# The first expert team's upward products, expert by expert, with the ring slots given back one at a time

## The chip, the cores and the metric

The kernel runs on one core of one Trainium2 chip. The metric is the time of one execution on the device in microseconds (us); lower is better.

## What is computed

One layer on 256 tokens of width 2048, all in float32: an attention and retention mixer, which the change does not touch, and then a mixture of experts. Each token chooses one of 4 groups and in it the best 2 of 8 experts, so there are 32 experts with three matrices each (`w1`, `w3`: 2048 x 512, `w2`: 512 x 2048), 12.6 MB an expert and about 403 MB in all. The part that matters, cut from the reference:

```
h = rms_norm(x, norm2_g)
a = jnp.einsum('nd,edf->nef', hf, w1)
b = jnp.einsum('nd,edf->nef', hf, w3)
y = jnp.einsum('nef,efd->nd', jax.nn.silu(a) * b * comb[..., None], w2)
```

`comb` is zero but for a token's two experts. The kernel computes each expert only for the tokens that chose it, in 32 slots.

## The kernel before

**Teams.** The experts are computed in 8 teams of 4 (`TEAM`), each expert with 32 token slots (`SLOTS`), so that a team fills 128 slots. The weights of a team come in 24 transfers of 2 MB (128 partitions x 4096 float32), numbered k = 0 to 23. Transfers 0 to 3 are the first half (q = 0) of `w1` of the four experts, 4 to 7 the first half of `w3`, 8 to 11 and 12 to 15 the second halves (q = 1) of `w1` and `w3`, and 16 to 23 are `w2` (two groups of four). They go into a ring of 8 slots; for the first team three further buffers (`extra`) hold transfers 8 to 10.

**The queue.** All of them are issued in this order by SyncE (L352, in `load`). Before each it waits for the semaphore `ring_used`, which counts transfers that TensorE has done with. In the first team transfer 11 waits for `ring_used` >= 1, transfer 12 for 2, ..., 18 for 8, and transfers 19 to 23 wait for 12 to 16; transfer k of a later team `it` waits for `it * 24 + k - 7`, so that of the second team, which is number 24 in the count of the whole stream, waits for 17.

**A team on TensorE.** `gather` picks the rows of the normalised input that belong to the slots by products with a 0/1 matrix `pick_p` (L1448, four parts j of four 128-column chunks; ScalarE copies each part to `h_e`, L703). `up` multiplies `h_e` by `w1` into bank 0 and by `w3` into bank 1: the stationary operand is 128 x 32 (the 32 slots of one expert), the moving one 128 x 512 (all inner columns of that expert). The four experts of the team write to four groups of 32 output partitions, so that four products with different weights are in the array side by side. Each product of float32 operands appears as two weight loads and two matmuls in the trace. The loop takes all four experts of a chunk before the next chunk, and gives back four transfers together:

```
last.then_inc(ring_used, TEAM)
```

ScalarE then makes the silu (L728, scaled by the slot's reciprocal root mean square, which TensorE gathers at L1442), VectorE the product `hm` (L1153), TensorE turns `hm` (L1499) and runs `down` (L1517) with `w2`, again four experts side by side. In the order of TensorE's program the gathering for the next team lies between a team's `up` and its `down` (`between`). The order for the first team, in `first_team`, is: `gather` 0 and 1, `up` q = 0, `gather` 2 and 3, `up` q = 1, `between`.

**The columns.** Row p*4+j of `w2` lies on partition p, so the inner columns of `hm` are read in four classes j, every fourth column, before they are turned:

```
hm.rearrange("p (j q) -> p j q", j=J), ps[:, 1, :].rearrange("p (q j) -> p j q", j=J)
```

**VectorE before the first gathering.** `pick_tokens(0)` makes `pick_p` (L1106), which is what `gather` waits for, after the ranks (L1093). The reciprocal of the root (L1110) comes after it.

Of the kernel before, what the change touches and what calls it, by code (L numbers as in the profile page):

```python
# [32 lines left out]
ALU = mybir.AluOpType  # L33
# [3 lines left out]
P = 128  # L37
SEQ, D = 256, 2048
TH = SEQ // P
C = D // P  # L40
# [6 lines left out]
J = FF // P  # L47
# [4 lines left out]
NB = 512  # L52
# [3 lines left out]
SLOTS = 32  # L56
TEAM = P // SLOTS
# [29 lines left out]
SSQ, RSTD, QKS, QKR, MU, VAR, M8, NEG, SUM, RCP, RETS, RETR, EPS_AT, SSQ2, RSTD2, SLOT_RSTD = (  # L87
    0, 2, 4, 24, 44, 48, 52, 68, 84, 100, 116, 132, 148, 150, 158, 160)
# [13 lines left out]
def build(nc, x, norm1_g, w_in, q_norm_g, k_norm_g, idx_k_ln_w, idx_k_ln_b, ret_norm_g, w_out,  # L102
          norm2_g, w_group, w_router, w1, w3, w2, consts, out):
    ctx = ExitStack()
    with ctx:
# [22 lines left out]
        side_buf = sb("side_buf", [P, 8192])  # L128
# [12 lines left out]
        st = sb("st", [P, 162])  # L141
# [69 lines left out]
        gate_T = side_buf[:, 4608:4864]  # L211
        e_sb = side_buf[:, 4864:5376]
        hm = side_buf[:, 5376:5888]
        hm_T = side_buf[:, 5888:6400].rearrange("p (j s) -> p j s", j=J)


# [15 lines left out]
        ring_used = sem("ring_used")  # L232
# [253 lines left out]
        def _(act):  # L486
# [231 lines left out]
            def slot_rstd(it):  # L718
                act.wait_ge(gather_done, it * 4 + 4)
                nc.scalar.copy(st[:, SLOT_RSTD:SLOT_RSTD + 1], ps[:, 7, 0:1]).then_inc(slot_rstd_ready, 1)  # L720

            slot_rstd(0)

            def activate(it):

                act.wait_ge(slot_rstd_ready, it + 1)
# [39 lines left out]
        def _(v):  # L766
# [322 lines left out]
                                    idxf[:, :, 1, 0:2].unsqueeze(3).broadcast_to([P, TH, 2, EXPERTS]), ALU.is_equal))  # L1089
            V.tensor_tensor(sel, oh[:, :, 0, :], oh[:, :, 1, :], ALU.add).then_inc(sel_ready, 1)  # L1090
            v.wait_ge(sel_ready, 1)
            v.wait_ge(ranks_done, 1)
            ordered(V.scalar_tensor_tensor(posm, ps[:, 1, 0:2 * EXPERTS].rearrange("p (t e) -> p t e", t=TH), 1.0, sel,  # L1093
                                           ALU.add, ALU.mult))
# [8 lines left out]
            def pick_tokens(g):  # L1103

                it, col = slots(posm, g)
                V.tensor_tensor(pick_p, col, it, ALU.is_equal).then_inc(pick_ready, 1)  # L1106

            pick_tokens(0)
            v.wait_ge(root_done, 2)
            V.reciprocal(st[:, RSTD2:RSTD2 + TH], st[:, RSTD2:RSTD2 + TH]).then_inc(rstd_ready, 1)  # L1110
            v.wait_ge(rstd_ready, 3)
            for th in range(TH):
                V.tensor_scalar(g_in[:, th, :], ps[:, 4 + th, EXPERTS:GATES], r2[th], None, ALU.mult)
                V.tensor_scalar(small[:, th, 0:1], top8[:, th, 0, 0:1], -1.0, r2[th], ALU.mult, ALU.mult)
# [21 lines left out]
            v.sem_inc(gate_turned, 1)  # L1136
            v.sem_inc(gate_T_ready, 1)

            def team(it, more=True, scattering=True):

                v.wait_ge(gate_turned, it + 1)
                i, col = slots(posm, it)
                V.tensor_tensor(gate_p, col, i, ALU.is_equal).then_inc(pick_step, 1)  # L1143
                v.wait_ge(pick_step, it + 1)
                V.tensor_tensor(gate_p, gate_p, slots(comb, it)[1], ALU.mult).then_inc(gate_ready, 1)
                v.wait_ge(gather_done, it * 4 + 4)
                if more:
                    pick_tokens(it + 1)
                if scattering:
                    add_scattered(it)  # L1150

                v.wait_ge(silu_done, it + 1)
                V.scalar_tensor_tensor(hm.rearrange("p (j q) -> p j q", j=J), ps[:, 1, :].rearrange("p (q j) -> p j q", j=J),  # L1153
                                       st[:, SLOT_RSTD:SLOT_RSTD + 1], e_sb.rearrange("p (q j) -> p j q", j=J),
                                       ALU.mult, ALU.mult).then_inc(hm_ready, 1)
# [14 lines left out]
                    xo = acc[:, th, n * NB:(n + 1) * NB]  # L1170
                    V.tensor_tensor(xo, xo, ps[:, 3 - s % 2, :], ALU.add).then_inc(added, 1)

            team(0, scattering=False)
            v.wait_ge(acc_ready, TH)
            with v.Fori(1, TEAMS - 1) as it:
                team(it)
# [11 lines left out]
        def _(pe):  # L1188
# [245 lines left out]
            mm(ps[:, 6, 0:EXPERTS], ones, sel[:, 0, :], start=True, stop=False)  # L1434
            mm(ps[:, 6, 0:EXPERTS], ones, sel[:, 1, :], start=False, stop=True).then_inc(totals_done, 1)

            def gather(g, j):

                if j == 3:
                    pe.wait_ge(rstd_ready, 3)  # L1440
                    for th in range(TH):
                        mm(ps[:, 7, 0:1], pick_p[:, th].rearrange("p e s -> p (e s)"), st[:, RSTD2 + th:RSTD2 + th + 1],  # L1442
                           start=(th == 0), stop=(th == TH - 1))
                for c in range(4 * j, 4 * j + 4):
                    cols = slice(c // 8 * 1024, (c // 8 + 1) * 1024)
                    for th in range(TH):
                        rows = xs[:, th, cols].rearrange("p (q c) -> p c q", c=8)[:, c % 8, :]
                        last = mm(ps[:, 2 + j % 2, (c % 4) * P:(c % 4 + 1) * P], rows,  # L1448
                                  pick_p[:, th].rearrange("p e s -> p (e s)"), start=(th == 0), stop=(th == TH - 1))
                last.then_inc(gather_done, 1)  # L1450
# [22 lines left out]
            def landed_now(it, k):  # L1473
                pe.wait_ge(landed[chunk_slot(k)], it * (16 * TEAM_CHUNKS // RING) + chunk_landed(k))
                return ring[:, chunk_slot(k), :]

            def up(it, q, here=None):

                pe.wait_ge(h_e_ready, it * 4 + (2 * q + 2))
                for up in range(2):  # L1480
                    ks = [(2 * q + up) * TEAM + m for m in range(TEAM)]
                    w = [here(k) if here else landed_now(it, k) for k in ks]
                    for cc in range(8):
                        c = 8 * q + cc
                        for m in range(TEAM):
                            part = slice(SLOTS * m, SLOTS * (m + 1))
                            last = mm(ps[part, up, :], h_e[:, c, part], w[m][:, cc * NB:(cc + 1) * NB],  # L1487
                                      start=(c == 0), stop=(c == C - 1))
                    last.then_inc(ring_used, TEAM)

            def ups(it):
                up(it, 0)
# [16 lines left out]
            def down(it, halves, here=None):  # L1509
                for half in halves:  # L1510
                    ks = [UP_CHUNKS + TEAM * half + m for m in range(TEAM)]
                    w = [here(k) if here else landed_now(it, k) for k in ks]
                    for j in (2 * half, 2 * half + 1):
                        for n in range(4):
                            for m in range(TEAM):
                                part = slice(SLOTS * m, SLOTS * (m + 1))
                                last = mm(ps[part, 4 + n, :], hm_T[:, j, part],  # L1517
                                          w[m][:, j % 2 * D + n * NB:j % 2 * D + (n + 1) * NB],
                                          start=(j == 0), stop=(j == J - 1))
                    last.then_inc(ring_used, TEAM)  # L1520

            def first_team():

                pe.wait_ge(pick_ready, 1)
                for j in range(2):
                    gather(0, j)
                up(0, 0, landed_first)
                for j in (2, 3):
                    pe.wait_ge(h_e_ready, j - 1)
                    gather(0, j)  # L1530
                up(0, 1, landed_first)
                between(0, landed_first)

            def team(it):
                ups(it)
                pe.wait_ge(added, it * 8 + 16)
                between(it)
# [91 lines left out]
```

## Time and profile before

| what | value |
|---|---|
| median of 3 runs | 1373.95 us (1373.59 to 1374.65) |
| the profiled execution, its own time | 1375.35 us |
| its span on the core | 1372.8 us |
| TensorE busy | 1041.9 us (76%) |
| VectorE, ScalarE busy | 332.1 us, 305.5 us |
| moved by DMA | 480.55 MB, 350 GB/s over the span |
| chain that ended last | DMA 47%, PE 47% |

The span is what the rows count from; the execution's own time holds 2.55 us more, outside the rows. The profiled execution is 1.40 us above the median. PE is TensorE, PEld its weight loads, DVE VectorE, ACT ScalarE, SPq the queue of SyncE. "x" before a number counts instructions.

### The profile page before, as it was taken

Reading aid. Unit: us, or ns where it says so; the run is one execution under the profiler, and the core shown is the slowest. Engines: PE = TensorE matmul, PEld = TensorE weight load, DVE = VectorE, ACT = ScalarE, POOL = GpSimd, SP = SyncE. Lnnn points to the kernel's source line nnn. Section 1 sums busy time; section 2 is a strip of 40 time slices with the busy share of each in tenths; the row PEclk is TensorE's granted clock in tenths of the full one; section 3 lists DMA queues with packets and bytes.
Section 4 is the critical chain, followed back from the end, with each engine's and each line's share of the span. In section 5 each row is a group of like instructions: output and inputs, shape, how many; then the busy total and the mean of one; then the engine's idle time right before and its main releaser. Section 6 shows DMA issues by size and latency. Waiting matters only on the chain.

```text
span 1372.8 us, 14551 instructions
## 1 busy us (share of the span) xinstructions
PE 1041.9 (76%) x5992; PEld 633.6 (46%) x5992; DVE 332.1 (24%) x496; ACT 305.5 (22%) x545; POOL 65.0 (5%) x47
## 2 busy tenths in 40 slices
PE   7999999999999886558576565847756683695547
PEld 6987888888888543115124111512511250161112
DVE  5457967545743200010010000001001000100101
ACT  6545555545543211001001100100100010010000
POOL 1000242500100010000000000000000000000000
PEclk9999999999999998689888877978878896898868
DMA  8745544554794899999999999999999999999997
GB/s 273 236 147 168 200 153 144 188 161 156 257 406 160 356 430 426 428 429 425 431 428 428 429 428 429 426 430 429 428 429 428 429 424 430 428 428 428 427 426 295
DMA packets 69467, 480.55 MB, mean 350 GB/s; under 512 B 4712, under 2 KB 8992, under 8 KB 44848
## 3 DMA queue, kind: packets, MB, share of 16 engines
q1 hardware_dynamic: 68896, 478.90, 85.6%
q0 software_dynamic: 528, 1.06, 0.3%
q8 instruction: 30, 0.49, 0.1%
q14 instruction: 13, 0.11, 0.0%
HBM read 477.84 MB, written 2.10 MB: 350 GB/s over the span
## 4 chain that ended last, share of the span: by engine, by line
DMA 47%; PE 47%; SPq 2%; DVE 2%; issue 1%; ACT 1%; ACTq 0%
DMA ring<-w_dram 47%; PE ps L1487 11%; PE ps L1239 9%; PE ps L1240 9%; PE ps L1241 9%; PE ps L1517 5%; SPq L352 2%; DVE w_lo L790 1%; PE ps L1255 1%; DMA xs<-x_dram 1%; PE ps L1577 1%; PE ps L1448 1%; PE ps L1349 0%; PE ps L1271 0%; PE ps L1565 0%
## 5 line engine op out<-in xcount | busy, mean ns | idle before, releaser
L1487 PE MATMUL ps<-ring,side_buf 128*32 128x512 f32 x2000 | 278.5, 709 | 255.5 <-DMA ring<-w_dram 254.3
L1487 PEld LDWEIGHTS ps<-ring,side_buf 128*32 128x32 f32 x2000 | 75.1, 128 | 452.3 <-issue 362.0
L1239 PE MATMUL ps<-w_hi,zT_hi 128*128 128x512 f32 (+2 forms) x576 | 221.8, 385 | 1.7 <-DVE w_lo L790 1.7
L1241 PE MATMUL ps<-w_hi,zT_lo 128*128 128x512 f32 (+2 forms) x576 | 218.7, 380 | 0.0
L1240 PE MATMUL ps<-w_lo,zT_hi 128*128 128x512 f32 (+2 forms) x576 | 218.7, 380 | 0.0
L790 DVE TENSOR_TENSOR w_lo<-raw_buf,w_hi 128x1024 fp32r<-128x1024 f32 (+2 forms) x144 | 181.2, 1277 | 143.4 <-ACT w_hi L512 142.8
L512 ACT CAST w_hi<-raw_buf 128x1024 fp32r<-128x1024 f32 (+2 forms) x144 | 143.6, 1016 | 107.1 <-PE ps L1241 101.0
L1517 PE MATMUL ps<-ring,side_buf 128*32 128x512 f32 x960 | 121.4, 663 | 44.2 <-DMA ring<-w_dram 43.1
L1163 DVE TENSOR_TENSOR buf_a<-buf_a,ps 128x512 f32<-128x512 f32 x56 | 38.5, 688 | 434.0 <-PE ps L1460 433.9
L728 ACT ACTIVATE side_buf<-ps,st 128x512 f32<-128x512 f32 x8 | 5.5, 687 | 549.0 <-PE ps L1487 549.0
L1448 PEld LDWEIGHTS ps<-const,xs 128*128 128x128 f32 x512 | 123.2, 335 | 6.8 <-issue 6.7
L1448 PE MATMUL ps<-const,xs 128*128 128x128 f32 x512 | 126.2, 406 | 0.0
L1239 PEld LDWEIGHTS ps<-w_hi,zT_hi 128*128 128x128 f32 x576 | 108.3, 188 | 23.4 <-DVE w_lo L790 3.2
L1241 PEld LDWEIGHTS ps<-w_hi,zT_lo 128*128 128x128 f32 x576 | 108.2, 188 | 20.4
L1240 PEld LDWEIGHTS ps<-w_lo,zT_hi 128*128 128x128 f32 x576 | 108.3, 188 | 19.0
L1517 PEld LDWEIGHTS ps<-ring,side_buf 128*32 128x32 f32 x960 | 35.0, 121 | 125.4 <-issue 125.1
L1153 DVE SCALAR_TENSOR_TENSOR side_buf<-ps,st,side_buf 128x512 f32<-128x512 f32 x8 | 9.2, 1149 | 244.6 <-ACT side_buf L728 244.6
L703 ACT ACTIVATE side_buf<-ps,g_col 128x128 f32<-128x128 f32 x128 | 36.5, 368 | 110.5 <-PE ps L1448 110.5
L1460 PE MATMUL ps<-side_buf 128*128 128x512 f32 x112 | 54.0, 619 | 0.0
L744 ACT COPY side_buf<-ps 128x512 f32<-128x512 f32 x28 | 14.4, 600 | 148.0 <-PE ps L1517 148.0
L1460 PEld LDWEIGHTS ps<-side_buf 128*128 128x128 f32 x112 | 17.3, 188 | 36.7 <-DVE buf_a L1163 27.5
L1143 DVE TENSOR_TENSOR const<-route,const 128x256 f32 (+1 forms) x8 | 3.4, 425 | 112.9 <-PE ps L1505 112.0
(191 smaller groups left out, 491.4 us busy)
## 6 DMA issues: line engine op xcount, KB each, us to landing
ring<-w_dram SPq DMA_DIRECT2D x185, 2048.0 KB, 20.0
raw_buf<-w_in_dram SPq DMA_DIRECT2D x48, 1024.0 KB, 5.0
raw_buf<-w_out_dram SPq DMA_DIRECT2D x16, 1024.0 KB, 6.7
spare<-w_dram SPq DMA_DIRECT2D x2, 2048.0 KB, 18.3
ring<-w_dram SPq DMA_DIRECT2D x4, 1024.0 KB, 14.9
ring<-w_dram SPq DMA_DIRECT2D x8, 512.0 KB, 18.8
raw_buf<-w_in_dram SPq DMA_DIRECT2D x4, 608.0 KB, 7.1
raw_buf<-w_in_dram SPq DMA_DIRECT2D x4, 576.0 KB, 3.8
```

Of the source, the lines that this page charges most:

```text
L352: sp.dma_start(dst, src.rearrange("o p n -> (o p) n")).then_inc(signal, 16)
L512: nc.scalar.copy(split(w_hi, u), raw(u)).then_inc(hi_done, 1)
L703: last = nc.scalar.activation(h_e[:, c, :], ps[:, 2 + j % 2, cc * P:(cc + 1) * P], ACT.Copy, scale=g2_col[:, c:c + 1])
L790: V.tensor_tensor(split(w_lo, u), raw(u), split(w_hi, u).bitcast(F32), ALU.subtract).then_inc(lo_done, 1)
L1163: V.tensor_tensor(xo, xo, ps[:, 3 - s % 2, :], ALU.add).then_inc(added, 1)
L1239: mm(b, zh[:, c, t], wh, start=(c == 0), stop=False)
L1240: mm(b, zh[:, c, t], wl, start=False, stop=False)
L1241: last = mm(b, zl[:, c, t], wh, start=False, stop=(c == C - 1))
L1448: last = mm(ps[:, 2 + j % 2, (c % 4) * P:(c % 4 + 1) * P], rows, pick_p[:, th].rearrange("p e s -> p (e s)"), start=(th == 0), stop=(th == ...
L1460: mm(ps[:, 3 - s % 2, :], gate_T[:, th * P:(th + 1) * P], y_sb[:, n * NB:(n + 1) * NB], start=True, stop=True).then_inc(scattered, 1)
L1487: last = mm(ps[part, up, :], h_e[:, c, part], w[m][:, cc * NB:(cc + 1) * NB], start=(c == 0), stop=(c == C - 1))
L1517: last = mm(ps[part, 4 + n, :], hm_T[:, j, part], w[m][:, j % 2 * D + n * NB:j % 2 * D + (n + 1) * NB], start=(j == 0), stop=(j == J - 1))
```

## The change

In the first team only:

- The upward products go by `up_serial`. It takes one transfer after the other: one expert's half matrix, eight chunks, and for each chunk the four classes g of inner columns. Each class is a product of its own with a 128 x 32 stationary operand and a 128 x 128 moving one, which reads every fourth float32 of the weights (a step of 16 bytes), and the class decides which group of 32 output partitions it goes to. All four have the same stationary operand. So a transfer takes 32 products of 128 columns where it took 8 of 512. After each transfer `ring_used` rises by 1.
- The first product waits for the first part of `h_e` only, the fifth chunk for the second.
- The output now has the class in the partitions and the expert in the columns, so `hm` is a plain product on contiguous columns, and `down` reads the turned `hm` through `hm_T_serial`.
- A partition no longer belongs to one expert's slot, so the slot's scale can't be applied at the silu. It is put into `pick_p`: VectorE takes the reciprocal of the root ahead of the ranks, and multiplies `pick_p` by it (one more 128 x 256 instruction behind L1106). The slot scale is set to 1.0, and the gathering of it (L1442) and its copy (L720) fall away for this team.

The diff:

```diff
--- before.py
+++ after.py
@@ -211,6 +211,7 @@
         gate_T = side_buf[:, 4608:4864]
         e_sb = side_buf[:, 4864:5376]
         hm = side_buf[:, 5376:5888]
+        hm_T_serial = side_buf[:, 5888:6400].rearrange("p (m j s) -> p m j s", m=TEAM, j=J)
         hm_T = side_buf[:, 5888:6400].rearrange("p (j s) -> p j s", j=J)
 
 
@@ -719,8 +720,6 @@
                 act.wait_ge(gather_done, it * 4 + 4)
                 nc.scalar.copy(st[:, SLOT_RSTD:SLOT_RSTD + 1], ps[:, 7, 0:1]).then_inc(slot_rstd_ready, 1)
 
-            slot_rstd(0)
-
             def activate(it):
 
                 act.wait_ge(slot_rstd_ready, it + 1)
@@ -1089,6 +1088,10 @@
                                     idxf[:, :, 1, 0:2].unsqueeze(3).broadcast_to([P, TH, 2, EXPERTS]), ALU.is_equal))
             V.tensor_tensor(sel, oh[:, :, 0, :], oh[:, :, 1, :], ALU.add).then_inc(sel_ready, 1)
             v.wait_ge(sel_ready, 1)
+            V.memset(st[:, SLOT_RSTD:SLOT_RSTD + 1], 1.0).then_inc(slot_rstd_ready, 1)
+            v.wait_ge(root_done, 2)
+            V.reciprocal(st[:, RSTD2:RSTD2 + TH], st[:, RSTD2:RSTD2 + TH]).then_inc(rstd_ready, 1)
+            v.wait_ge(rstd_ready, 3)
             v.wait_ge(ranks_done, 1)
             ordered(V.scalar_tensor_tensor(posm, ps[:, 1, 0:2 * EXPERTS].rearrange("p (t e) -> p t e", t=TH), 1.0, sel,
                                            ALU.add, ALU.mult))
@@ -1105,10 +1108,10 @@
                 it, col = slots(posm, g)
                 V.tensor_tensor(pick_p, col, it, ALU.is_equal).then_inc(pick_ready, 1)
 
-            pick_tokens(0)
-            v.wait_ge(root_done, 2)
-            V.reciprocal(st[:, RSTD2:RSTD2 + TH], st[:, RSTD2:RSTD2 + TH]).then_inc(rstd_ready, 1)
-            v.wait_ge(rstd_ready, 3)
+            it, col = slots(posm, 0)
+            ordered(V.tensor_tensor(pick_p, col, it, ALU.is_equal))
+            r2_wide = st[:, RSTD2:RSTD2 + TH].unsqueeze(2).unsqueeze(3).broadcast_to([P, TH, TEAM, SLOTS])
+            V.tensor_tensor(pick_p, pick_p, r2_wide, ALU.mult).then_inc(pick_ready, 1)
             for th in range(TH):
                 V.tensor_scalar(g_in[:, th, :], ps[:, 4 + th, EXPERTS:GATES], r2[th], None, ALU.mult)
                 V.tensor_scalar(small[:, th, 0:1], top8[:, th, 0, 0:1], -1.0, r2[th], ALU.mult, ALU.mult)
@@ -1136,7 +1139,7 @@
             v.sem_inc(gate_turned, 1)
             v.sem_inc(gate_T_ready, 1)
 
-            def team(it, more=True, scattering=True):
+            def team(it, more=True, scattering=True, serial=False):
 
                 v.wait_ge(gate_turned, it + 1)
                 i, col = slots(posm, it)
@@ -1150,6 +1153,9 @@
                     add_scattered(it)
 
                 v.wait_ge(silu_done, it + 1)
+                if serial:
+                    V.tensor_tensor(hm, e_sb, ps[:, 1, :], ALU.mult).then_inc(hm_ready, 1)
+                    return
                 V.scalar_tensor_tensor(hm.rearrange("p (j q) -> p j q", j=J), ps[:, 1, :].rearrange("p (q j) -> p j q", j=J),
                                        st[:, SLOT_RSTD:SLOT_RSTD + 1], e_sb.rearrange("p (q j) -> p j q", j=J),
                                        ALU.mult, ALU.mult).then_inc(hm_ready, 1)
@@ -1170,7 +1176,7 @@
                     xo = acc[:, th, n * NB:(n + 1) * NB]
                     V.tensor_tensor(xo, xo, ps[:, 3 - s % 2, :], ALU.add).then_inc(added, 1)
 
-            team(0, scattering=False)
+            team(0, scattering=False, serial=True)
             v.wait_ge(acc_ready, TH)
             with v.Fori(1, TEAMS - 1) as it:
                 team(it)
@@ -1434,9 +1440,9 @@
             mm(ps[:, 6, 0:EXPERTS], ones, sel[:, 0, :], start=True, stop=False)
             mm(ps[:, 6, 0:EXPERTS], ones, sel[:, 1, :], start=False, stop=True).then_inc(totals_done, 1)
 
-            def gather(g, j):
-
-                if j == 3:
+            def gather(g, j, slot_rstd=True):
+
+                if j == 3 and slot_rstd:
                     pe.wait_ge(rstd_ready, 3)
                     for th in range(TH):
                         mm(ps[:, 7, 0:1], pick_p[:, th].rearrange("p e s -> p (e s)"), st[:, RSTD2 + th:RSTD2 + th + 1],
@@ -1474,12 +1480,11 @@
                 pe.wait_ge(landed[chunk_slot(k)], it * (16 * TEAM_CHUNKS // RING) + chunk_landed(k))
                 return ring[:, chunk_slot(k), :]
 
-            def up(it, q, here=None):
+            def up(it, q):
 
                 pe.wait_ge(h_e_ready, it * 4 + (2 * q + 2))
                 for up in range(2):
-                    ks = [(2 * q + up) * TEAM + m for m in range(TEAM)]
-                    w = [here(k) if here else landed_now(it, k) for k in ks]
+                    w = [landed_now(it, (2 * q + up) * TEAM + m) for m in range(TEAM)]
                     for cc in range(8):
                         c = 8 * q + cc
                         for m in range(TEAM):
@@ -1487,6 +1492,22 @@
                             last = mm(ps[part, up, :], h_e[:, c, part], w[m][:, cc * NB:(cc + 1) * NB],
                                       start=(c == 0), stop=(c == C - 1))
                     last.then_inc(ring_used, TEAM)
+
+            def up_serial(q):
+
+                for up in range(2):
+                    for m in range(TEAM):
+                        w = landed_first((2 * q + up) * TEAM + m)
+                        slots = slice(SLOTS * m, SLOTS * (m + 1))
+                        for cc in range(8):
+                            c = 8 * q + cc
+                            if up == m == 0 and cc % 4 == 0:
+                                pe.wait_ge(h_e_ready, c // 4 + 1)
+                            cols = w[:, cc * NB:(cc + 1) * NB].rearrange("p (f g) -> p g f", g=J)
+                            for g in range(J):
+                                last = mm(ps[SLOTS * g:SLOTS * (g + 1), up, m * P:(m + 1) * P], h_e[:, c, slots], cols[:, g, :],
+                                          start=(c == 0 and m == 0), stop=(c == C - 1 and m == TEAM - 1))
+                        last.then_inc(ring_used, 1)
 
             def ups(it):
                 up(it, 0)
@@ -1514,7 +1535,8 @@
                         for n in range(4):
                             for m in range(TEAM):
                                 part = slice(SLOTS * m, SLOTS * (m + 1))
-                                last = mm(ps[part, 4 + n, :], hm_T[:, j, part],
+                                h_j = hm_T_serial[:, m, j, :] if here else hm_T[:, j, part]
+                                last = mm(ps[part, 4 + n, :], h_j,
                                           w[m][:, j % 2 * D + n * NB:j % 2 * D + (n + 1) * NB],
                                           start=(j == 0), stop=(j == J - 1))
                     last.then_inc(ring_used, TEAM)
@@ -1523,12 +1545,12 @@
 
                 pe.wait_ge(pick_ready, 1)
                 for j in range(2):
-                    gather(0, j)
-                up(0, 0, landed_first)
+                    gather(0, j, slot_rstd=False)
+                up_serial(0)
                 for j in (2, 3):
                     pe.wait_ge(h_e_ready, j - 1)
-                    gather(0, j)
-                up(0, 1, landed_first)
+                    gather(0, j, slot_rstd=False)
+                up_serial(1)
                 between(0, landed_first)
 
             def team(it):
```

## Rows read from the trace of the kernel before

**Rows 1.** The page, the 40 slices: clock of TensorE, DMA share and GB/s.
```profile
PEclk9999999999999998689888877978878896898868
DMA  8745544554794899999999999999999999999997
GB/s 273 236 147 168 200 153 144 188 161 156 257 406 160 356 430 426 428 429 425 431 428 428 429 428 429 426 430 429 428 429 428 429 424 430 428 428 428 427 426 295
```
**Rows 2.** The chain that ended last in order of time: start, duration, what.
```profile
451.96 7.93 PE ps L1448 x32
459.92 1.15 ACT side_buf L703 x4
461.11 13.98 PE ps L1487 x128
475.11 21.33 DMA ring<-w_dram
496.58 8.74 PE ps L1487 x64
```
**Rows 3.** Half microseconds of the DMA: stretch, length, clock, DMA share, GB/s.
```profile
463.50:464.00 0.50, 1.00 0.84 360
464.00:464.50 0.50, 1.00 0.24 98
464.50:465.00 0.50, 1.00 0.00 0
...
468.50:469.00 0.50, 1.00 0.00 0
469.00:469.50 0.50, 1.00 1.79 360
469.50:470.00 0.50, 1.00 0.31 98
470.00:470.50 0.50, 1.00 0.58 164
470.50:471.00 0.50, 1.00 1.01 426
```
**Rows 4.** Timeline of all engines, from the first team's start to the second's loads.
```profile
448.78 0.30 ACT L489 ACTIVATE st<-st 128x2 f32<-128x2 f32 x1 [0.26 <-DVE st L1083]
449.76 0.22 DVE L1090 TENSOR_TENSOR route<-route 128x64 f32<-128x64 f32 x1
450.04 0.69 PE L1432 MATMUL ps<-route,const 128*128 128x64 f32 x2 [2.99 <-DVE route L1090]
451.22 0.23 DVE L1093 SCALAR_TENSOR_TENSOR route<-ps,route 128x64 f32<-128x64 f32 x1 [1.23 <-PE ps L1433]
466.22 0.43 DVE L1143 TENSOR_TENSOR const<-route,const 128x256 f32<-128x256 f32 x1 [0.88 <-DVEq L1136]
466.68 0.43 DVE L1145 TENSOR_TENSOR const<-const,route 128x256 f32<-128x256 f32 x1
468.25 38.84 SPq L352 DMA_DIRECT2D ring<-w_dram  x13
474.98 4.07 PE L1448 MATMUL ps<-const,xs 128*128 128x128 f32 x16
479.26 4.05 PE L1448 MATMUL ps<-const,xs 128*128 128x128 f32 x16
522.92 7.07 PE L1517 MATMUL ps<-ring,side_buf 128*32 128x512 f32 x64
530.21 54.74 SPq L352 DMA_DIRECT2D ring<-w_dram  x14
```
**Rows 5.** Timeline of the weight loads while four experts' products run side by side.
```profile
484.57 0.12 PEld L1487 LDWEIGHTS ps<-spare,side_buf 128*32 128x32 f32 x2
484.59 0.11 PEld L1487 LDWEIGHTS ps<-ring,side_buf 128*32 128x32 f32 x1
```
**Rows 6.** Single lines: duration in ns, least, median, most, for weight loads.
```profile
L1255 PEld LDWEIGHTS ps<-const,flat x84: 138/141/144, 83.4 to 365.9; 128*128 128x128 f32 x84
L1335 PEld LDWEIGHTS ps<-const,xs x32: 196/211/220, 390.4 to 444.6; 128*128 128x128 f32 x32
L1305 PEld LDWEIGHTS ps<-p_t,flat x48: 187/192/193, 203.5 to 249.3; 128*128 128x128 f32 x48
L1448 PEld LDWEIGHTS ps<-const,xs x512: 312/336/339, 452.0 to 1226.7; 128*128 128x128 f32 x171
```
**Rows 7.** Timeline of one dense run with contiguous operands.
```profile
236.93 1.95 PE L1305 MATMUL ps<-p_t,flat 128*128 128x128 f32 x16
```

## The prediction

> **What bounds the kernel now.** I read the page's slices first. In the last 26 of 40 slices the DMA share is 9 tenths or more at some 428 GB/s, with TensorE's clock often below full [rows 1]: from about 470 us on the kernel waits for weights. Such a time moves only if the stream of 2 MB transfers starts earlier or stops somewhere. At 428 GB/s one transfer of 2.097 MB takes 4.9 us. The chain of waits says the same: behind the first upward products come a transfer of 21.33 us, then products, then the next wait [rows 2]. Before that there is a hole in the stream, and the half-microsecond windows measure it: the data of transfer 10 ends at about 464.1 us, nothing moves to 469.0, and the flow is whole only at 470.5 [rows 3]. Summing the shortfall gives 5.6 us; the stream behaves as if it restarted at 469.75, 1.5 us behind the issue at 468.25 [rows 3, 4]. The issue comes at half of the 13.98 us of products [rows 2]: all four experts are given back together, 7 us after the start.
>
> Where does the stream have slack next? Transfers 11 to 23 are 13 x 4.9 = 63.7 us, so the data of 24, the second team's first, would begin at 469.75 + 63.7 = 533.45 us. Its issue is at 530.21, the moment TensorE has done half of the first `down`, 522.92 + 7.07 = 529.99 [rows 4]. So TensorE may be only 533.45 - 1.5 - 530.2 = 1.7 us later before the stream breaks there. That is the second place the change touches, since all upward products of the first team lie ahead of it.
>
> **The change, part by part.** I work with one unknown, T, the time that TensorE takes for the products of one transfer. Before, eight take 13.98 us: T = 1.75 [rows 2].
>
> VectorE. The memset, the reciprocal and its wait run from 449.98, when `sel` is done, while TensorE makes the ranks, from 450.04 until VectorE can go on at 451.22 [rows 4]. The root that the reciprocal needs is done at 449.08 [rows 4]. Some 0.4 us fits in 1.2 us of cover: nothing; without the cover it would be those 0.4 us. The added product on `pick_p` is not covered: `gather` stands right behind it. The same pair on the same shape starts 0.46 us apart (L1143, L1145) [rows 4]: +0.46 us.
>
> Start. The gathering of two parts then ends at 451.96 + 7.93 + 0.46 = 460.35 [rows 2]. The first product no longer waits for the second ScalarE copy (1.15 us and its start, to 461.11), only its fifth chunk does, at 461.57; with T above 2.4 this is hidden, with T = 1.75 it costs some 0.3 us. So the serial products start at 460.35 and transfer 0 is given back at 460.35 + T.
>
> Gathering of parts 2 and 3: from 474.98 to 479.26 + 4.05 = 483.31, without the 0.2 us that L1442 puts between the two [rows 4]: 8.1 us. The second half starts behind it at once. The upward products end, if no data is late, at 460.35 + 8T + 8.1 + 8T = 468.5 + 16T. Before, the second `w3` group ran from 496.58 to 505.3 [rows 2], because its data landed then.
>
> Behind them the program is the old one: from 505.3 to the start of `down` at 522.92 17.6 us (gathering for the second team and the turnings), and 7.07 us for half of it [rows 2, 4], in all 24.7. The silu and `hm` run under that gathering; `hm` reads contiguously now, which shortens covered work: nothing. Transfer 24 is issued 0.2 us later and its data counts 1.5 us after that: 468.5 + 16T + 24.7 + 0.2 + 1.5 = 494.9 + 16T. Against 533.45 this gives the term that decides:
>
> shift = 16T - 38.5 us, and no better than 464.1 - 469.75 = -5.7 us, which is the whole hole.
>
> Break-even is T = 2.4 us. Up to T = 2.05 the gain is whole; above it each 0.1 us costs 1.6 us. Once the stream runs again, the ring is empty and TensorE has the slack of the later teams as before, so the shift stays to the end.
>
> **What is T?** A transfer is 32 products, 64 records, in four column groups, so 16 rounds of four. Nothing in the trace is a narrow product side by side, nor a moving operand with a step. From below: the same columns stream as before, 128 in place of 512, and the round would take a quarter of the old 13.98/32 = 0.437: T = 1.75. For the step there are rows on the stationary side. A turning (one weight load, one pass) of contiguous data has a load of 141 ns, a float32 product with two passes 192: a pass over 128 columns is 51 ns, the fixed part 90. With a step of 16 bytes (L1335) the load takes 211, with one of 32 bytes (L1448) and two passes 336: 121 and 246/2 = 123 ns a pass [rows 6]. So a read with a step of 16 bytes goes 2.4 times slower, the same as one of 32, and it shows in the pace too: 16 records in 4.07 us against 16 contiguous ones in 1.95 [rows 4, 7]. The new moving operand has just this step, in 128 columns and two passes a record. If it reads like the stationary one, a round takes 0.246 us even with four groups side by side: T = 16 x 0.246 = 3.94. I take it: it is the nearest row that has the step, and I see nothing that makes the moving side quicker. From above, if the four groups also take turns, T = 15.8.
> The Trainium skill (SBUF — State Buffer, the note on cachelines) says that SBUF has 16-byte lines and that an access wants two hits in a line for full bandwidth, for any reader. By that rule the moving operand pays as well and T is near 3.9; if it did not hold on the moving side, T would be 1.75 and the result the gain of 5.7. The trace agrees for weight loads (211 against 141 ns); no row shows the moving side.
>
> Sum with T = 3.94: 16 x 3.94 - 38.5 = +24.5 us. The gain at the hole is inside it: transfer 0 is back at 464.3, and the hole shrinks to some 2 us. But then transfer 19 waits for 11, at 468.5 + 12 x 3.94 = 515.8, where the stream has run out at about 505, and transfer 24 waits a second time, at 556.5 + 1.5 against 542. The profiled execution would go from 1375.35 to 1399.9 us, its span from 1372.8 to 1397.3; against the median of 1373.95 that is 1398.5.
>
> **The rivals.**
> *The columns alone count (T up to 2.2).* No penalty for the step on the moving side, loads covered. For it: loads start some 10 ns apart when they are queued [rows 5], the groups did run side by side, and the moving operand may be buffered otherwise than weights. Against it: rows 6. Time: 1373.95 - 5.7 = 1368.3. It decides where T is below 2.4. Chance 0.22.
> *The rate of instructions (T 2.5 to 3.7).* 128 weight loads and matmuls a transfer; at T = 1.75 one each 14 ns. The densest lasting pace that the trace shows is 32 in 1.95 us, 61 ns each [rows 7], on a busy array, so it is no limit shown; the burst of 10 ns [rows 5] comes from a filled queue. Between these ends I take their geometric mean, 25 ns: T = 128 x 0.025 = 3.2, shift 16 x 3.2 - 38.5 = +12.7, 1386.7. Chance 0.18 for a T in this range (1375.5 to 1394.7). The Trainium skill (TensorE: Matmul & The Clock Gate, back-to-back issue gap) has a floor of about 25 ns between starts of matmuls; on matmuls alone it gives T = 1.6 and changes nothing, on loads as well it gives 3.2. No run here shows it.
> *No change that can be told (T 2.23 to 2.57).* The early give-back and the late second team cancel. Chance 0.04.
> *The groups don't run side by side (T over 4.3).* All four read the same weights' lines at once, with one stationary operand. At T = 5 it is +41.5 us, in turns +214. Against it: four streams at once before at full pace. Chance 0.10.
>
> **How the numbers follow.** The likeliest case, the step penalty with T from 3.7 to 4.3, has 0.46: 1394.7 to 1404, predicted 1398.5. The range has to reach the gain, 1367.5, as that case has 0.22, and ends at 1404; outside is the last rival and little else. Within 0.2% (2.7 us, about what a measurement of this kernel can tell from no change) 0.04, faster 0.22, slower 0.46 + 0.18 + 0.10 = 0.74.
>
> **What would show it.** In the profile after: `up_serial` in 31.5 us for 8 transfers, with matmul records of a group 0.25 us apart (0.11 if the columns alone count); the first issue behind transfer 10 at 464.5; windows with a DMA share near 0 around 506 to 517 and 543 to 558; the second team's first load issued at 556; the same intervals as before from there on. If the DMA share stays at 1 from 464 on, the gain rival is right. The prediction is wrong if T is not 3.7 to 4.3, or if the later teams' slack takes the shift back.

## The result, and the profile after

The changed kernel takes 1394.11 us (median of 4 runs, 1391.80 to 1394.51) against 1374.01 before (median of 4 runs beside it): a ratio of 1.0146, 95% interval 1.0134 to 1.0158, or +20.1 us. The forecast was 1398.5, with a range from 1367.5 to 1404. The profiled execution took 1394.51 us, its span 1392.3, which is 19.5 more than the 1372.8 of the kernel before.

The page's slices of the changed kernel, clock of TensorE, DMA share and GB/s, stand beside [rows 1]:

```profile
PEclk9999999999999999688888968988887896887878
DMA  8745644545786975999999999999999999999997
GB/s 277 245 139 167 196 139 151 201 160 192 255 348 228 407 320 240 430 428 427 427 429 429 429 428 428 429 427 428 429 429 428 429 425 428 428 428 428 427 427 296
```

The stream is whole only two slices later than before. The chain that ended last, by start, duration and what, answers to [rows 2]:

```profile
451.68 7.92 PE ps L1454 x32
459.59 29.61 PE ps L1508 x488
489.20 7.82 PE ps L1454 x32
497.02 29.57 PE ps L1508 x502
526.59 11.62 PE ps L1454 x48
...
544.23 13.99 PE ps L1539 x128
...
559.68 35.30 DMA ring<-w_dram
```

L1508 is the serial product. Eight transfers take 29.6 us, so T = 3.70 us. Where the old chain has a wait for data behind the first products, this one is TensorE from 459.6 to 558, but for 1.7 us before `down`. DMA windows of the changed kernel (stretch, length, clock, share, GB/s), the counterpart of [rows 3]:

```profile
463.00:464.00 1.00, 1.00 0.43 180
464.00:465.00 1.00, 1.00 1.07 229
465.00:466.00 1.00, 1.00 0.60 213
466.00:467.00 1.00, 1.00 0.92 393
...
500.00:505.00 5.00, 1.00 0.88 374
505.00:510.00 5.00, 1.00 0.05 16
510.00:515.00 5.00, 1.00 0.46 141
515.00:520.00 5.00, 1.00 1.02 429
...
540.00:545.00 5.00, 1.00 0.00 0
545.00:550.00 5.00, 1.00 0.01 3
550.00:555.00 5.00, 1.00 0.50 147
555.00:560.00 5.00, 1.00 1.00 429
```

Of the old hole, which cost 5.6 us of the stream, about 1.7 us are left: that is what these four windows lack of 428 GB/s. Two new holes stand in its place. One lasts from about 505 to 513; the other begins at about 538 (the window from 538 to 539 has 66 GB/s) and lasts to about 553. The forecast had put them at 506 to 517 and 543 to 558. The timeline of the changed kernel has the steps that the prediction spoke of [rows 4]:

```profile
450.74 0.43 DVE L1112 TENSOR_TENSOR const<-route,const 128x256 f32<-128x256 f32 x1
451.19 0.43 DVE L1114 TENSOR_TENSOR const<-const,st 128x256 f32<-128x256 f32 x1
451.68 7.92 PE L1454 MATMUL ps<-const,xs 128*128 128x128 f32 x32 [0.46 <-DVE const L1114]
463.48 11.40 SPq L353 DMA_DIRECT2D ring<-w_dram  x4
551.52 1.56 SPq L353 DMA_DIRECT2D ring<-w_dram  x3
```

The second product on `pick_p` starts 0.45 us behind the first, and the gathering waits for it. The first load behind transfer 10 is issued at 463.5 instead of 468.25, as wished. But transfer 24 is issued at 551.5 instead of 530.2; with the 1.5 us of restart its data begins at 553.0, against 533.45: +19.6 us, which is the whole difference of the spans.

### The profile page after: what moved, and what is told of

The parts are those of the page before. It is cut to its first block, busy times and chain, and to the rows that moved or that the text cites. A ratio compares the mean times of both kernels' runs of the same rounds, so it can differ in the third digit from the quotient of the medians.

```text
span 1392.3 us, 16073 instructions
## 1 busy us (share of the span) xinstructions
PE 1065.6 (77%) x6756; PEld 666.9 (48%) x6756; DVE 332.0 (24%) x498; ACT 305.4 (22%) x544; POOL 65.0 (5%) x47
## 4 chain that ended last, share of the span: by engine, by line
PE 51%; DMA 43%; SPq 2%; DVE 2%; issue 1%; ACT 1%; ACTq 0%; DVEq 0%
DMA ring<-w_dram 43%; PE ps L1492 9%; PE ps L1245 9%; PE ps L1247 8%; PE ps L1246 8%; PE ps L1539 5%; PE ps L1508 4%; PE ps L1454 2%; SPq L353 2%; DVE w_lo L789 1%; PE ps L1261 1%; PE ps L1599 1%; DMA xs<-x_dram 1%; PE ps L1355 0%; PE ps L1277 0%
## 5 line engine op out<-in xcount | busy, mean ns | idle before, releaser
L1492 PE MATMUL ps<-ring,side_buf 128*32 128x512 f32 x1792 | 245.1, 709 | 255.8 <-DMA ring<-w_dram 255.8
L1492 PEld LDWEIGHTS ps<-ring,side_buf 128*32 128x32 f32 x1792 | 66.0, 128 | 434.3 <-issue 338.0
L1539 PE MATMUL ps<-ring,side_buf 128*32 128x512 f32 x960 | 120.4, 660 | 40.4 <-DMA ring<-w_dram 39.3
L1169 DVE TENSOR_TENSOR buf_a<-buf_a,ps 128x512 f32<-128x512 f32 x56 | 38.5, 688 | 431.8 <-PE ps L1466 431.7
L1539 PEld LDWEIGHTS ps<-ring,side_buf 128*32 128x32 f32 x960 | 34.4, 120 | 121.1 <-issue 120.7
L1508 PE MATMUL ps<-ring,side_buf 128*32 128x128 f32 x832 | 48.3, 409 | 0.0
L743 ACT COPY side_buf<-ps 128x512 f32<-128x512 f32 x28 | 14.4, 600 | 141.3 <-PE ps L1539 141.3
L1508 PEld LDWEIGHTS ps<-ring,side_buf 128*32 128x32 f32 x832 | 36.7, 128 | 11.0
```

The source lines that it names most:

```text
L1508: last = mm(ps[SLOTS * g:SLOTS * (g + 1), up, m * P:(m + 1) * P], h_e[:, c, slots], cols[:, g, :], start=(c == 0 and m == 0), stop=(c == C ...
L1539: last = mm(ps[part, 4 + n, :], h_j, w[m][:, j % 2 * D + n * NB:j % 2 * D + (n + 1) * NB], start=(j == 0), stop=(j == J - 1))
```

## The experiments

**The step or the rate of instructions?** T = 3.70 fits both theories: it is near the 3.94 of the step, and it is 29 ns for each of 128 instructions. Four kernels were run to tell them apart. `contig` is the changed kernel with

```
- cols = w[:, cc * NB:(cc + 1) * NB].rearrange("p (f g) -> p g f", g=J)
+ cols = w[:, cc * NB:(cc + 1) * NB].rearrange("p (g f) -> p g f", g=J)
```

> The changed kernel with one difference: the class g of the moving operand is the g-th contiguous quarter of the 512 columns, no longer every fourth column (so hm's columns no longer match w2's rows; the number, shapes and order of all instructions stay). The changed kernel took T = 3.70 us a transfer. If the 16-byte step is what costs (my theory), T falls to 1.75 us, the hole in the stream nearly closes and the time is 1374 - 5.7 = 1368.3 us. If the rate of instructions costs (128 in 3.70 us, 29 ns each), T stays 3.7 and the time 1394. A value between says that both do.

Measured: 1378.37 us, ratio to before 1.0041 (1.0027 to 1.0055). Neither end of the expectation came out: 16 us of the change's 20 go with the step, and 4.6 us stay against the kernel before, run beside it (1373.80). Lines of its TensorE timeline, in the first half:

```profile
461.28 6.09 PE L1508 MATMUL ps<-ring,side_buf 128*32 128x128 f32 x212 [0.22 <-ACT side_buf L704]
469.32 3.70 PE L1508 MATMUL ps<-ring,side_buf 128*32 128x128 f32 x128 [1.95 <-issue]
475.52 5.16 PE L1508 MATMUL ps<-ring,side_buf 128*32 128x128 f32 x128 [2.50 <-issue]
```

and in the second:

```profile
497.67 3.70 PE L1508 MATMUL ps<-ring,side_buf 128*32 128x128 f32 x128 [1.33 <-issue]
504.15 3.70 PE L1508 MATMUL ps<-ring,side_buf 128*32 128x128 f32 x128 [2.78 <-issue]
510.63 1.51 PE L1508 MATMUL ps<-ring,side_buf 128*32 128x128 f32 x45 [2.78 <-issue]
```

Inside a burst the pace is nearly that of the columns: 3.70/128 = 29 ns a record, 1.85 us a transfer, where the kernel before had 1.75. But a burst between two stops is 128 records, and the next begins 6.2 to 6.5 us after the last began; what lies between is "issue", nothing that the profile shows. The burst of 5.16 us has a granted clock of 0.50 (1.2 GHz) from 475.5 to 478.5, behind a stop of 2.50 us. 128 matmuls with their weight loads are 256 instructions. Over a whole half, stops included, eight transfers take 22.1 us (459.98 to 482.08) and 22.3 us (489.83 to 512.14): T = 2.8 on average.

`step8` has the step of 8 bytes (halves of 256, every second column):

> The changed kernel with a step of 8 bytes in the moving operand (every second column of a half of 256, so again hm's columns no longer match w2's rows). If two uses of each 16-byte line are enough, T is that of contiguous columns, 1.75 us, and the time 1368. If every step costs alike, T stays 3.7 us and the time 1394. If it goes by lines touched, half of the 16-byte step's, T is 1.85 to 2.0 us.

Measured: 1380.0 us in one run, not 1368, because the stops of `contig` are there as well (1.0 to 2.6 us of "issue" each). By line, duration in ns (least, median, most), of the changed kernel (16 bytes), `contig` and `step8`:

```profile
L1508 PE MATMUL ps<-spare,side_buf x128: 405/408/433, 500.6 to 507.8; 128*32 128x128 f32 x128
```
```profile
L1508 PE MATMUL ps<-spare,side_buf x128: 272/273/273, 492.0 to 495.4; 128*32 128x128 f32 x128
```
```profile
L1508 PE MATMUL ps<-spare,side_buf x128: 273/276/283, 493.4 to 497.0; 128*32 128x128 f32 x128
```

A record lasts 3 ns longer with a step of 8 bytes and 135 ns longer with one of 16 bytes. In pace, 128 records of a burst take 3.87 to 3.90 us with 8 bytes against 3.70 with contiguous columns, some 5% more; with 16 bytes they take 7.4, twice as long. The Trainium skill (SBUF — State Buffer, the note on cachelines) asks for two uses of each 16-byte line: the trace agrees on the moving side now, 273, 276 and 408 ns. The same note also calls 4 fp32 a stride that is free; a step of 4 float32, which is 16 bytes, isn't free here.

`wide_step` has the step alone, in the kernel before, for the first team (cut from its diff):

```
+ V.scalar_tensor_tensor(hm, ps[:, 1, :], st[:, SLOT_RSTD:SLOT_RSTD + 1], e_sb,
+                        ALU.mult, ALU.mult).then_inc(hm_ready, 1)
...
+ if here:
+     cols = cols.rearrange("p (f g) -> p g f", g=J)
```

> The kernel before, with the 16-byte step alone: in the first team the four experts still run side by side in products of 512 columns, but the columns are read class by class (step of 16 bytes) and hm contiguously; same number of instructions as before. If the step costs, T is 3.7 us: first group given back at 461.1 + 14.8 = 475.9, upward products end at 461.1 + 29.6 + 9.5 + 29.6 = 529.8 us, transfer 24's data at 529.8 + 24.7 + 1.7 = 556.2 against 533.45, so +22.8 us: 1397. If the rate of instructions costs, nothing changes: 1374.

Measured: 1395.79 us, ratio 1.017 (1.0153 to 1.0187), +22.0 us in the medians for 22.8. The second half of its upward products, in the chain:

```profile
499.24 29.01 PE ps L1494 x128
```

That is T = 3.63 with no instruction more than before (it was 1.75). So with the step a product takes twice its time, narrow or wide: 29.01/32 = 0.907 us a round of 512 columns against 0.437. The trace holds one thing more. At the start of this half, from 499.0 to 502.4 us, the granted clock was 0.51 (1.2 GHz), behind 1.2 us in which TensorE waited for ScalarE, and from 502.5 on it was 1.00. The records last the same in both stretches:

```profile
L1494 PE MATMUL ps<-spare,side_buf x8: 1077/1079/1087, 499.2 to 502.0; 128*32 128x512 f32 x8
```
```profile
L1494 PE MATMUL ps<-spare,side_buf x12: 1079/1079/1079, 502.9 to 507.4; 128*32 128x512 f32 x12
```

So under this step TensorE's clock did not set the pace.

`by_four` is the changed kernel with the give-back undone:

```
-                         last.then_inc(ring_used, 1)
+                     last.then_inc(ring_used, TEAM)
```

> The changed kernel with the give-back undone: ring_used rises by four behind the fourth transfer. By my sum the late transfer 24 alone sets the time: its issue goes by TensorE, so the early give-back bought nothing and the time stays 1394 us within 0.2%, although the first hole grows by some 11 us (data again at 460 + 14.8 + 1.7 = 476.8). The rival, that the stream's holes add up, gives 1394 + 11 = 1405 us.

Measured: 1393.57 us, ratio to before 1.0145 (1.0128 to 1.0162); the changed kernel's 1.0146 lies inside. Its DMA windows:

```profile
465.00:470.00 5.00, 1.00 0.03 8
470.00:475.00 5.00, 1.00 0.01 3
475.00:480.00 5.00, 1.00 0.59 197
```

The stream idles for twelve us here, and the time does not change. So in the changed kernel the early give-back earns nothing: what it closes in front opens again before transfer 24.

**What makes the stops?** `quarters` computes the reference with contiguous columns; the row order in which the first team's `w2` is loaded takes over what the step did (cut from its diff):

```
+ w2_first = w2.rearrange("l e (j p) n -> (l e) p j n", j=J)
```

> A version that computes the reference with contiguous columns: the changed kernel with the g-th quarter of the columns in group g, and the first team's w2 loaded with row j*128+p on partition p (two pieces of 8 KB a partition in place of one of 16 KB). The run with mismatched rows took 1378.4 us, its products in bursts of exactly 128 records (1.85 us a transfer) with stalls of 2 to 2.8 us between them. If the w2 pieces cost nothing, 1378.4 again; if they cost, up to 2 us more.

Measured: 1379.85 us (1377.35 to 1380.55), ratio 1.004 (1.0025 to 1.0055), as `contig` within the intervals; a cost of the smaller pieces up to some 2 us would not show. It is the change without its step, and still slower than before.

`contig_quiet` is `contig` with the stream kept still beside the first eight transfers:

```
- sp.wait_ge(ring_used, k - RING + 1 if k >= 2 * RING + EXTRA else k - RING - EXTRA + 1)
+ sp.wait_ge(ring_used, k - RING + 1 if k >= 2 * RING + EXTRA else RING)
```

> The contiguous changed kernel, but no transfer of the ring from 11 on is issued before the first eight are used: no data moves beside the first eight transfers' products once transfer 10 has landed at about 466. My theory is that TensorE runs out of instructions (128 records are 256 instructions with their loads) and that fetching them is slow beside the data. If the data is in their way, the stalls between the bursts shrink to below 1 us in this stretch and T is near 1.85; if fetching is slow by itself, they stay at 2 to 2.8 us and T at 2.6.

Measured: 1380.4 us in one run. What it was run for is the timeline of TensorE, with the DMA's windows:

```profile
460.96 1.08 PE L1508 MATMUL ps<-ring,side_buf 128*32 128x128 f32 x32
462.26 13.31 PE L1508 MATMUL ps<-ring,side_buf 128*32 128x128 f32 x480 [0.22 <-ACT side_buf L704]
```
```profile
468.00:469.00 1.00, 1.00 0.06 16
469.00:470.00 1.00, 1.00 0.00 0
470.00:471.00 1.00, 1.00 0.00 0
471.00:472.00 1.00, 1.00 0.06 16
```

In this half no stop is left: 512 records in some 14.4 us with one wait for ScalarE. In the second half of the same run, where the stream is back at 415 to 442 GB/s, the stops are back too (the burst of 4.77 us falls partly into a stretch at half clock):

```profile
491.21 4.01 PE L1508 MATMUL ps<-ring,side_buf 128*32 128x128 f32 x128 [1.39 <-issue]
497.96 4.77 PE L1508 MATMUL ps<-ring,side_buf 128*32 128x128 f32 x109 [2.75 <-issue]
```

And where no data moves, 16 KB pass about every 3.5 us (16 GB/s for one us). The DMA view has them on an instruction queue, 3 packets with 0.05 MB from 466 to 480:

```profile
q8 instruction: 3, 0.05, 1.3%
```

The pages tell whose packets these are. They count the packets of a whole execution, here for `before`, `half_classes`, `first_half`, `second_half` and the changed kernel in turn:

```profile
q8 instruction: 30, 0.49, 0.1%
q8 instruction: 32, 0.52, 0.2%
q8 instruction: 33, 0.54, 0.2%
q8 instruction: 33, 0.54, 0.2%
q8 instruction: 36, 0.59, 0.2%
```

On the same pages TensorE has 504, 760, 760 and 1528 instructions (matmuls and weight loads) more than in `before`, which is 2, 3, 3 and 6 times 256 but for 8; the packets are 2, 3, 3 and 6 more. So what is added on queue 8 is TensorE's instructions, 256 in each packet of 16 KB. Asked in windows of 0.1 us, the DMA view also gives the start of each packet, which can be set beside the end of each stop:

| run and half | packet starts | stop ends | later by |
|---|---|---|---|
| `contig`, first | 466.9, 473.2, 479.2 | 469.32, 475.52, 481.45 | 2.4, 2.3, 2.3 |
| `contig`, second | 495.4, 501.8, 508.0 | 497.67, 504.15, 510.63 | 2.3, 2.4, 2.6 |
| `contig_quiet`, second | 488.8, 495.6 | 491.21, 497.96 | 2.4, 2.4 |

Each of these eight stops ends 2.3 to 2.6 us after a packet has started, whatever its own length (0.77 to 2.78 us); the twelve of `quarters` and `step8` lie between 2.2 and 2.6. Without data beside them (`contig_quiet`, first half) packets start 3.3 to 3.9 us apart, which keeps up with TensorE; beside the data 5.9 to 6.8 us. The packet itself lasts 0.93 to 0.96 us there and 0.93 to 1.09 us here, so it is the start of the packets that comes late, and not their own time that grows.

`half_classes` leaves out classes 2 and 3 of the contiguous kernel (`for g in range(J // 2)`), and with them half of the upward products of the first team and their instructions:

> The contiguous changed kernel with only classes 0 and 1 computed (half of the products and half of the instructions left out, two column groups idle). If the supply of instructions (256 each 6.5 us) makes the stalls, 64 instructions a transfer go through at array pace, T = 1.75 to 1.85 without stalls, and the time is that of the gain: 1374 - 5.7 = 1368.3 us. If the stalls come from the array, from narrow products or from waits, they stay and the time is 1378.

Measured: 1368.32 us, ratio 0.9959 (0.9944 to 0.9975). The products of the first half:

```profile
462.65 13.29 PE ps L1508 x240
```

There is no stop, and T is 1.8 (14.6 us for eight transfers), beside a full stream. This is also the gain that the change aimed at: with TensorE fast enough the early give-back is worth 5 us (1368.32 against 1373.36 beside it).

**Is the sum right?** `first_half` and `second_half` put the serial products, with the step, into one half only and `up` as before into the other. The formula with the measured T = 3.70 gave both expectations.

> The changed kernel with the serial products only in the first half (q = 0); the second half runs the four experts side by side in products of 512 columns (so the two halves no longer add up to the right sums). By my sum with T = 3.70: first half from 460.35 to 490, gathering to 498.1, second half 14 us to 512.1, then 24.7 + 1.7: transfer 24's data at 538.5 against 533.45, so +5 us: 1379. If the loss were an effect of the whole program and not of this sum, half of it, +10: 1384.

Measured: 1379.15 us, ratio 1.0043 (1.0026 to 1.0060).

> The changed kernel with the serial products only in the second half (q = 1; again the sums don't match). First half as before, a little later (461.6 to 475.6), gathering and the copy to 484.9, serial second half 29.6 us to 514.5, then 26.4: 540.9 against 533.45, so +7.5 us: 1381.5. Together with the other half alone it should show that the two don't add up to 20 by halves: each has the slack of the stream once.

Measured: 1380.36 us, ratio 1.0047 (1.0030 to 1.0063). They cost 5.5 and 6.8 us against before (1373.61 beside them), 12.3 together where both at once cost 20.1. The products of one half take 29.6 us for 14.0, which is 15.6 us more; 5.5 and 6.8 of these show. Both halves together take 31.2 us more, and 20.1 show. So 9 to 11 us fall into slack, once, however the delay is made up; the formula has 38.5 - 16 x 1.75 = 10.5 us for it.

**One edit alone.** `early_start` is the kernel before with the waits for `h_e` split in the first team (cut from its diff; the wait at the head of `up` falls away there):

```
+ if here is not None and up == 0 and cc % 4 == 0:
+     pe.wait_ge(h_e_ready, c // 4 + 1)
```

> The kernel before with one edit of the change alone: the first product waits for the first part of h_e only, the fifth chunk for the second. Products start at 459.9 in place of 461.1 and the first group comes back up to 1.2 us earlier, so the hole shrinks by that: 1374 - 1.2 = 1372.8 us, 0.1%, which only the trace will tell for certain. Rival: TensorE stops in the middle for the same copy and nothing moves.

Measured: 1372.29 us, 11 runs, ratio 0.9994 (0.9985 to 1.0003), which is not to be told from no change. In its trace the products start at 459.76 and the issue behind them at 466.82 instead of 468.25:

```profile
459.76 13.92 PE ps L1490 x128
```
```profile
466.82 118.33 SPq L352 DMA_DIRECT2D ring<-w_dram  x29
```

So the hole is 1.4 us shorter, of which 0.1 comes from an earlier start of the gathering. Of the versions that compute the whole layer it is the only one that may be faster than before, by some 0.1%.

## Why the prediction held

**The two places.** The argument was that the stream gains at most 5.7 us at its first hole and breaks again at transfer 24. Both show in the windows after, `by_four` shows that only the second sets the time, and `half_classes` that the first is worth its 5 us when TensorE keeps up. The 1.7 us of slack at transfer 24 were not measured by themselves; the sum that contains them came out within 1.1 us.

**The formula.** 16T - 38.5 gives +20.7 with the measured T of 3.70; measured +19.6 at transfer 24 and +20.1 in the medians. With T = 3.70 put in after the result, it gave +5 and +7.5 for the serial products in one half, where +5.5 and +6.8 were measured, and +22.8 for `wide_step`, where +22.0 were. For `contig` with its average T of 2.8 it gives +6 for +4.6, and for `half_classes` the whole gain of -5.7 for -5.0. The other terms: gathering 7.8 for 8.1 us, the way from the products to `down` 17.64 for 17.6, and the start 0.76 us earlier than 460.35, because all that lies ahead ran some 0.75 us earlier in this execution. VectorE's part was +0.45 for +0.46, and the reciprocal was hidden.

**T, the term that was mis-sized.** 3.94 was taken from weight loads with the same step; the products took 3.70 (3.63 when wide). The mechanism is the one named: a product with a step of 16 bytes takes 0.227 to 0.231 us a round of 128 columns, where the loads' rows gave 0.246. That is 6 to 8% less. At transfer 24 the forecast was 4.9 us too high (+24.5 for +19.6): 3.8 of them are 16 times the 0.24 of T, 0.8 the earlier start and 0.3 the gathering. Against the median it was 4.4 too high.

**How near it was.** The prediction had named T from 3.7 to 4.3 as its likeliest case, and called itself wrong outside. T came out at 3.70, on the edge, and the median of 1394.11 us lies just below that case's 1394.7 to 1404 and inside the 1375.5 to 1394.7 of the rate of instructions. So the result by itself does not favour the step over that rival, and the range of 1367.5 to 1404 held the gain as well as the loss. It is `contig` and `wide_step`, run afterwards, that show the step as the cause.

**The rivals.** "The columns alone count" is out: the step doubles the product. "The rate of instructions" was not what set this time, since the pace under the step needs 256 instructions in 7.4 us and they come in 6.5. But it was right as a second limit behind the first: with the step gone T is 2.8 on average and the change still loses 4.6 us. My way of putting it was off. It is no floor for each instruction (in a burst they go at 14.5 ns each, and the 25 ns that I took as a mean of two ends would have made T = 3.2 there); it is a supply of 256 at a time. That this supply comes out at 24 to 25 ns an instruction beside full data is a coincidence: neither of the two ends, 10 and 61 ns, had to do with it. Nor was 61 ns the densest lasting pace in the old trace: the upward products themselves have 256 instructions in 13.98 us, 55 ns each. Four groups side by side held throughout; in turns T would have been 15.8.

**What stays open.** That TensorE stops for want of instructions, whose packets start late beside the data, rests on five things: the bursts of 128 pairs, the stops' going with half of the instructions, their going and coming back with the data inside one run, the count of one packet for 256 instructions, and the nearly constant 2.2 to 2.6 us from a packet's start to the end of a stop. No record names the fetch as what TensorE waited for, and none shows what holds a packet back before it starts. Why `contig` has a longer first burst in each half (244 and 211 records) I take for instructions fetched during the gathering; a packet does start at 456.0 and one at 484.9, in the two gatherings, but nothing was changed to try it. A version of the whole layer that has the early give-back with fewer instructions was not found.

## What to carry to other kernels

Giving a buffer back earlier is worth the hole that it closes only if the work that was rearranged for it stays within the slack of the next place where the stream waits; sum up to there, not to the first release. Before products are cut into narrower ones with a stepped moving operand, look for a row with that step anywhere in the trace, the weight loads included, and put the permutation elsewhere (here in the row order of `w2`; `quarters` shows no cost that could be told from `contig`). And count instructions: a limit hidden behind the first can take back what curing the first gives.

## What was not expected of the hardware

TensorE ran out of work in steps: beside a stream of some 428 GB/s it got 256 instructions (128 weight loads and matmuls each) every 6.2 to 6.5 us, with the data still it ran 512 pairs in 14.4 us without a stop. That is 24 to 25 ns for each instruction beside full data, and this code of narrow products took them at 14.5 ns each inside a burst. A burst went at 29 ns a pair, where the columns alone, in the wide products before, took 27, so the loads cost next to nothing of their own in it; the Trainium skill (TensorE: Matmul & The Clock Gate, back-to-back issue gap) has about 25 ns between starts of matmuls, and these 29 ns lie above it.

A step of 8 bytes in the moving operand is nearly free (276 against 273 ns a record, 5% in the pace of a burst); one of 16 bytes adds 135 ns to a record of 128 columns and takes twice the time. With it a record of 512 columns lasted 1079 ns in the median at a granted clock of 0.51 and of 1.00 alike (`wide_step`).
